# Decay sums of the scan: broadcast by transfers instead of by TensorE

## The reference

```python
a_cs = jnp.cumsum((dt * a).reshape(b, c, t, g, e), axis=2)
seg = a_cs[:, :, :, None] - a_cs[:, :, None, :]
decay = jnp.exp(jnp.where(lower, seg, -jnp.inf))
cb = jnp.einsum('bclgn,bcsgn->bclsg', Cc, Bc)
y_diag = jnp.einsum('bclsge,bcsgep->bclgep', cb[..., None] * decay, X)
y_off = jnp.einsum('bclgn,bcgepn->bclgep', Cc, s_in) * jnp.exp(a_cs)[..., None]
```

## Time and profile before

| | us |
|---|---|
| median of 3 runs | 1684.28 |
| all runs | 1684.26 to 1684.72 |
| profiled execution | 1684.64 |
| its span | 1682.9 |
| PE busy | 1659.0 |
| DVE busy | 1001.9 |
| ACT busy | 679.8 |
| POOL busy | 687.4 |

### The profile page before, as it was taken

The page is one execution under the profiler, slowest core; times in us unless marked ns, Lnnn a source line. Parts: engine busy times, 40 slices in busy tenths (PEclk is TensorE's granted clock), DMA queues, the critical chain, the costliest instruction groups (busy, mean ns, idle before and its releaser), DMA issues.

```text
span 1682.9 us, 20420 instructions
## 1 busy us (share of the span) xinstructions
PE 1659.0 (99%) x8004; PEld 1316.8 (78%) x8004; DVE 1001.9 (60%) x1387; ACT 679.8 (40%) x932; POOL 687.4 (41%) x339
## 2 busy tenths in 40 slices
PE   7999999999999999999999999999999999999999
PEld 5777787878778888888877777788777788888887
DVE  5589859778774545422236898596788654545100
ACT  5445553344443333332244555533543433333221
POOL 3432223233445555554443222232334455555443
PEclk9999999999999999999999999999999999999999
DMA  5532111212223232322224221112123223222233
GB/s 167 129 96 74 62 63 63 76 63 64 87 88 100 88 100 88 100 92 94 91 88 126 85 73 63 63 63 76 63 66 96 89 88 100 89 100 90 93 99 107
DMA packets 43231, 147.34 MB, mean 88 GB/s; under 512 B 5152, under 2 KB 5920, under 8 KB 43136
## 3 DMA queue, kind: packets, MB, share of 16 engines
q1 hardware_dynamic: 42752, 145.28, 26.9%
q0 software_dynamic: 384, 0.75, 0.4%
HBM read 143.17 MB, written 2.85 MB: 87 GB/s over the span
## 4 chain that ended last, share of the span: by engine, by line
PE 89%; DVE 6%; issue 2%; ACT 1%; POOL 1%; DMA 0%; SPq 0%; DVEq 0%
PE banks L1080 27%; PE banks L1082 26%; PE banks L1081 26%; PE banks L1172 2%; PE banks L1151 2%; PE banks L1160 2%; PE banks L1255 1%; DVE sb_w_lo L747 1%; PE banks L1268 1%; PE banks L1227 1%; PE banks L1131 1%; DVE sb_e L822 1%; PE banks L1241 1%; PE banks L1211 0%; DVE sb_squares L735 0%
## 5 line engine op out<-in xcount | busy, mean ns | idle before, releaser
L360 POOL TENSOR_TENSOR sb_w_lo<-sb_w_raw,sb_w_hi 128x1024 fp32r<-128x1024 f32 x202 | 490.4, 2428 | 633.1 <-ACT sb_w_hi L453 633.1
L1080 PE MATMUL banks<-sb_h_hi,sb_w_hi 128*128 128x512 f32 x1360 | 558.2, 410 | 16.1 <-POOL sb_w_lo L360 10.7
L453 ACT ACTIVATE sb_w_hi<-sb_w_raw 128x1024 fp32r<-128x1024 f32 x258 | 272.6, 1057 | 671.4 <-PE banks L1082 665.1
L1082 PE MATMUL banks<-sb_h_hi,sb_w_lo 128*128 128x512 f32 x1360 | 537.3, 395 | 0.0
L1081 PE MATMUL banks<-sb_h_lo,sb_w_hi 128*128 128x512 f32 x1360 | 537.1, 395 | 0.0
L1080 PEld LDWEIGHTS banks<-sb_h_hi,sb_w_hi 128*128 128x128 f32 x1360 | 256.5, 189 | 99.5 <-issue 36.9
L1081 PEld LDWEIGHTS banks<-sb_h_lo,sb_w_hi 128*128 128x128 f32 x1360 | 256.9, 189 | 61.8 <-issue 6.9
L1082 PEld LDWEIGHTS banks<-sb_h_hi,sb_w_lo 128*128 128x128 f32 x1360 | 256.5, 189 | 60.1
L1045 DVE TENSOR_TENSOR banks<-banks,sb_rstd 128x512 f32<-128x512 f32 x88 | 61.5, 699 | 144.0 <-PE banks L1082 135.7
L1080 PE MATMUL banks<-sb_ff_hi,sb_w_hi 128*128 128x512 f32 x352 | 138.9, 395 | 0.0
L1082 PE MATMUL banks<-sb_ff_hi,sb_w_lo 128*128 128x512 f32 x352 | 138.9, 395 | 0.0
(11 more groups left out here) (199 smaller groups left out, 2326.9 us busy)
## 6 DMA issues: line engine op xcount, KB each, us to landing
sb_w_raw<-w_in SPq DMA_DIRECT2D x88, 512.0 KB, 3.4
sb_w_raw<-w_up SPq DMA_DIRECT2D x88, 512.0 KB, 3.3
sb_w_raw<-w_out SPq DMA_DIRECT2D x32, 512.0 KB, 3.4
sb_w_raw<-w_down SPq DMA_DIRECT2D x32, 512.0 KB, 3.3
sb_bias_t<-bias_rows SPq DMA_DIRECT2D x16, 448.0 KB, 6.0
sb_w_raw<-w_down SPq DMA_DIRECT2D x16, 384.0 KB, 3.0
sb_x_stream<-x_t SPq DMA_DIRECT2D x4, 512.0 KB, 6.7
out_t<-sb_x_stream SPq DMA_DIRECT2D x8, 256.0 KB, 3.5
```

The lines of the kernel that those rows point to most:

```text
L360: g.tensor_tensor(WLO[:, n % 2, :], W[:, n % 2, :], WHI[:, n % 2, :].bitcast(F32), ALU.subtract).then_inc(w_lo.handle, 1)
L453: sc.activation(WHI[:, n % 2, :], W[:, n % 2, :], ACT.Copy).then_inc(w_hi.handle, 1)
L1080: mm(out, whi, hhi, start=start, stop=False)
L1082: return mm(out, wlo, hhi, start=False, stop=stop)
```

## The change

The rows of sums (and, exponentiated once by ScalarE for all heads, their exponentials) are stored to a buffer in HBM, `sum_rows`, at slot 4 of SyncE's order. SyncE then reads each head's two rows back into all 128 partitions of `head_e(h)` (`head_rows`, 512 KB), behind the weights of the slot two further on, and for each pair the exponentials of its four rows, each into 64 partitions of `EA` (`pair_exps`, two transfers of 192 KB). `row_sums` and its matmuls go, and with them the selectors, the high and low parts of the sums, and the exponential of L606. `seg` becomes eight operations of 128 columns, one for each direction and chunk, each of which subtracts the chunk's column and bounds in one. `HEAD_E` gets a fourth buffer, made of two pieces of 2 KB.

```diff
-    HEAD_E = (E[:, 0, :, :], E[:, 1, :, :], SQ[:, :, :])
+    HEAD_E = (E[:, 0, :, :], E[:, 1, :, :], SQ[:, :, :], rm["spread"][:, 0:16:15, :])
...
+        def store_rows():
+            sp.wait_ge(*cs_row.at(1))
+            sp.dma_start(sum_rows[0, :, :], T[0:2 * DIR, 0, :]).then_inc(rows_stored.handle, 16)
+            sp.wait_ge(*cs_exp.at(1))
+            sp.dma_start(sum_rows[1, :, :], ER[0:2 * DIR, :]).then_inc(rows_stored.handle, 16)
+
+        def head_rows(h):
+            grp, n = h // 8, h % 8
+            if h == 0:
+                sp.wait_ge(*rows_stored.at(32))
+                sp.wait_ge(*at_pv.at(UNITS))
+            if n % 4 == 2:
+                sp.wait_ge(*st_mm.at(6 * grp + 6))
+            if h == 3:
+                sp.wait_ge(*cb_mm.at(1))
+            if h >= 4:
+                sp.wait_ge(*y_mm.at(2 * ((h - 4) // 2) + 2))
+            rows = bass.AP(sum_rows.tensor, h * SEQ, [[0, P], [DIR * SEQ, 2], [1, SEQ]])
+            sp.dma_start(head_e(h), rows).then_inc(rows_landed[h % 4].handle, 16)
+
+        def pair_exps(t):
+            if t >= 2:
+                sp.wait_ge(*y_read.at(t - 1))
+            for d in range(2):
+                rows = bass.AP(sum_rows.tensor, (2 * DIR + DIR * d + 2 * t) * SEQ + (P, 0)[d], [[SEQ, 2], [0, 64], [1, SEQ - P]])
+                sp.dma_start(EA[:, t % 2, d, :], rows).then_inc(ea_landed[t % 2].handle, 16)
...
+                slot = pos - POS["sc", 0]
+                if slot == 4:
+                    store_rows()
+                if slot - 2 in ROWS_AT:
+                    head_rows(ROWS_AT[slot - 2])
+                if slot - 1 in PAIR_AT:
+                    pair_exps(PAIR_AT[slot - 1])
...
-                    act.wait_ge(*seg_read.at(h + 1))
-                    if h >= 4:
-                        act.wait_ge(*y_read.at(h // 2 - 1))
-                    sc.activation(EA[half, (h // 2) % 2, :, :].rearrange("p d l -> p (d l)"),
-                                  BANK[half, 2:4, :].rearrange("p b s -> p (b s)")[:, P:P + 768], ACT.Exp).then_inc(ea_done.handle, 1)
...
-                    sc.activation(CS[0:64, :], BANK[0:64, 2, :], ACT.Copy).then_inc(cs_hi.handle, 1)
+                    sc.activation(ER[0:64, :], BANK[0:64, 2, :], ACT.Exp).then_inc(cs_exp.handle, 1)
...
         def seg(h):
...
-            v.tensor_tensor(head_e(h).rearrange("p d (c l) -> p d c l", l=P),
-                            BANK[:, 2:4, :].rearrange("p d (c l) -> p d c l", l=P), columns, ALU.subtract).then_inc(seg_read.handle, 1)
-            dve.wait_ge(*seg_read.at(h + 1))
-            v.tensor_scalar(head_e(h), head_e(h), 80.0, None, ALU.min).then_inc(seg_done.handle, 1)
+            dve.wait_ge(*rows_landed[h % 4].at(16 * (h // 4 + 1)))
+            for d in range(2):
+                for c in range(QT):
+                    at = slice(P * c, P * c + P)
+                    ins = v.tensor_scalar(head_e(h)[:, d, at], head_e(h)[:, d, at], AS[:, c, column(d, h):column(d, h) + 1], 80.0,
+                                          ALU.subtract, ALU.min)
+            ins.then_inc(seg_done.handle, 1)
...
-            dve.wait_ge(*ea_done.at(2 * t + 2))
+            dve.wait_ge(*ea_landed[t % 2].at(32 * (t // 2 + 1)))
...
-                    dve.wait_ge(*cs_hi.at(1))
-                    v.tensor_tensor(CS[64:128, :], BANK[0:64, 2, :], CS[0:64, :].bitcast(F32), ALU.subtract).then_inc(cs_lo.handle, 1)
...
-                if k == KT // 2 and head is not None:
-                    row_sums(head)
...
-        def row_sums(h):
...
-            for d in range(2):
-                ins = mm(bank(2 + d), SEL[:, column(d, h):column(d, h) + 1].to_broadcast([P, P]), CS[:, :], start=True, stop=True)
-            ins.then_inc(ab_mm.handle, 1)
```

More of the change, by code:

```diff
@@ L159, in build_trunk @@
     con = {n: CON[:, i, :] for i, n in enumerate(CONSTS)}
-    SEL = sb("selectors", [P, 64], F32R)
     PAR = sb("params", [P, DEPTH, PA_N])
@@ L195, in build_trunk @@
                 ("x_tok", 40, [P, QT, 512], F32), ("s_in", 48, [P, 2, 3, SEQ], F32), ("b_tok", 60, [P, QT, P], F32),
-                ("cs", 62, [P, SEQ], F32R), ("exp_cs", 64, [P, 2, 2, 384], F32), ("cb", 70, [P, 2, SEQ], F32),
+                ("exp_rows", 62, [P, SEQ], F32), ("spread", 32, [P, 16, SEQ], F32), ("exp_cs", 64, [P, 2, 2, 384], F32), ("cb", 70, [P, 2, SEQ], F32),
                 ("e", 74, [P, 2, 2, SEQ], F32), ("mh_sc", 82, [P, 4, SEQ], F32R), ("ml_sc", 90, [P, 4, SEQ], F32R),
@@ L208, in build_trunk @@
     QHI, QLO, KHI, KLO = (rm[n] for n in ("q_high", "q_low", "k_high", "k_low"))
-    XT, SIN, BT, CS, EA, CB, E = (rm[n] for n in ("x_tok", "s_in", "b_tok", "cs", "exp_cs", "cb", "e"))
-    HEAD_E = (E[:, 0, :, :], E[:, 1, :, :], SQ[:, :, :])
+    XT, SIN, BT, ER, EA, CB, E = (rm[n] for n in ("x_tok", "s_in", "b_tok", "exp_rows", "exp_cs", "cb", "e"))
+    HEAD_E = (E[:, 0, :, :], E[:, 1, :, :], SQ[:, :, :], rm["spread"][:, 0:16:15, :])
     SCC, CX, SCA, SCP, Z = (rm[n] for n in ("sc_c", "sc_cx", "sc_acc", "sc_prod", "z"))
@@ L228, in build_trunk @@
     scratch = nc.dram_tensor("bias_rows", [HEADS, COPIES, REL], F32).ap()
+    sum_rows = nc.dram_tensor("sum_rows", [2, 2 * DIR, SEQ], F32).ap()
     con_landed, setup_landed = sem("con_landed"), sem("setup_landed")
@@ L233, in build_trunk @@
     x_stored = sem("x_stored")
-    sel_done, eps_done = sem("sel_done"), sem("eps_done")
+    eps_done = sem("eps_done")
+    rows_stored = sem("rows_stored", 32)
+    rows_landed = [sem(f"rows_landed{i}", 64) for i in range(4)]
+    ea_landed = [sem("ea_landed0", 128), sem("ea_landed1", 128)]
     bias_mm, bias_row = sem("bias_mm"), sem("bias_row")
@@ L258, in build_trunk @@
         sem(n, 1) for n in ("dt_tr", "dt_x", "dt_e", "dt_w", "dt_ln", "a_exp", "dt_done", "lndt_done", "da_done"))
-    cs_mm, cs_row, cs_hi, cs_lo, cs_tr, cs_col, dec_mm, dec_exp, ws_done = (
-        sem(n, 1) for n in ("cs_mm", "cs_row", "cs_hi_done", "cs_lo_done", "cs_tr", "cs_col", "dec_mm", "dec_exp", "ws_done"))
+    cs_mm, cs_row, cs_exp, cs_tr, cs_col, dec_mm, dec_exp, ws_done = (
+        sem(n, 1) for n in ("cs_mm", "cs_row", "cs_exp", "cs_tr", "cs_col", "dec_mm", "dec_exp", "ws_done"))
     tok_tr, tok_copied = sem("tok_tr", 10), sem("tok_copied", 10)
     cb_mm, cb_done, xs_done, st_mm, sin_done = sem("cb_mm", 2), sem("cb_done", 4), sem("xs_done", 12), sem("st_mm", 12), sem("sin_done", 12)
-    ab_mm, seg_read, seg_done, e_done, ea_done, g_done, y_mm = (
-        sem(n, SSD_HEADS) for n in ("ab_mm", "seg_read", "seg_done", "e_done", "ea_done", "g_done", "y_mm"))
+    seg_done, e_done, g_done, y_mm = (
+        sem(n, SSD_HEADS) for n in ("seg_done", "e_done", "g_done", "y_mm"))
     gs_done = sem("gs_done", SSD_HEADS // 2)
@@ L270, in head_e @@
     def head_e(h):
-        return HEAD_E[h % 8 % 3]
+        return HEAD_E[h % 4]
     def par(col, n=1):
@@ L601, in _ @@
                     h = ROWS_AT[s]
-                    half = slice(64 * (h % 2), 64 * (h % 2) + 64)
-                    act.wait_ge(*seg_read.at(h + 1))
-                    if h >= 4:
-                        act.wait_ge(*y_read.at(h // 2 - 1))
-                    sc.activation(EA[half, (h // 2) % 2, :, :].rearrange("p d l -> p (d l)"),
-                                  BANK[half, 2:4, :].rearrange("p b s -> p (b s)")[:, P:P + 768], ACT.Exp).then_inc(ea_done.handle, 1)
                     act.wait_ge(*seg_done.at(h + 1))
@@ L710, in setup @@
         def setup():
-            dve.wait_ge(con_landed.handle, 16)
-            v.tensor_tensor(SEL[:, :], con["ident"][:, 0:64], con["ident"][:, 64:128], ALU.add).then_inc(sel_done.handle, 1)
             for r in range(2):
@@ L855, in state_in @@
                 return
-            if grp:
-                dve.wait_ge(*t_read.at(4))
+            dve.wait_ge(*(t_read.at(4) if grp else rows_stored.at(32)))
             col = 64 + column(d, 8 * grp)
@@ L1103, in block_of, with tile @@
                 ins.then_inc(w_used.handle, 1)
-        def tile(kind, i, width=P, head=None):
+        def tile(kind, i, width=P):
             for k in range(KT):
-                if k == KT // 2 and head is not None:
-                    row_sums(head)
                 block_of(kind, i, k, width)
@@ L1197, in to_tokens @@
                 pe.wait_ge(*y_read.at(4))
-                pe.wait_ge(*ea_done.at(8))
-                pe.wait_ge(*seg_done.at(8))
             else:
-                pe.wait_ge(*cs_lo.at(1))
+                pe.wait_ge(*cs_exp.at(1))
                 pe.wait_ge(*cs_row.at(1))
@@ L1270, in from_states, with output_first @@
             ins.then_inc(yo_mm.handle, 1)
-        def output_first(m, head):
+        def output_first(m):
             s, b = weights("o1", m), tile_bank("o1", m)
             for k in range(KT):
-                if k == KT // 2 and head is not None:
-                    row_sums(head)
                 at = slice(P * k, P * k + P)
@@ L1345, in _ @@
                 if kind == "o1":
-                    output_first(i, ROWS_AT.get(s))
```

(3 more changed lines are left out.)

## The result

The changed kernel takes **1702.05 us** (median of 4 runs, 1700.33 to 1704.5) against 1684.3 for the kernel before on the same chip: ratio 1.0106, 95% interval 1.0088 to 1.0123. The change makes it slower, as forecast, but by 17.8 us where I had 9.0, and the time lies above the range (1673 to 1698). The profiled execution took 1700.33 us for a span of 1698.5, 15.6 more than before's 1682.9.

The account below looks back on a forecast made before the run. It took VectorE to run level with TensorE in the scans, so its work counts as much. Per layer -1.7 + 6.2 = +4.5 us, transfers 0, so +9.0 in all on 1684.64: 1693.6, put at 1693 us; range 1673 to 1698.

Parts of the forecast that it names:

- The passes, -15.0 us: Scans, TensorE: two matmuls a head fall away, 64 in all, 15.0 us over both layers, the most to win.
- VectorE runs level with TensorE: Scan stretches: VectorE arrives as TensorE needs it or up to 5 us before, so its work counts as much.
- `seg` at 1.68 us undisturbed: VectorE, each head: eight operations of 0.20 us plus a tail take 1.68 us, against 1.86 before.
- The port by turns: VectorE and GpSimd alternate by instruction, so eight short operations can lose a wait at each boundary; likeliest case, chance 0.48.
- slot 21 waiting for the z read-out: Group 1, TensorE: slot 21 waits for L1006's successor and starts at 376.9 us, four heads' gain gone.
- the walk: Old layer 0 times moved by the new seg: -1.7 us in group 0, +6.2 in group 1, +9.0 over both layers.
- head 15's `seg` at 7.55 us: End of group 1: beside four GpSimd operations it starts at 412.15 us and ends at 419.7.
- +6.2: Group 1, slot 25: `within` starts at 422.1 us instead of 415.93, 6.2 us later against the old course.
- The transfers: 23 MB of added reads of rows and exponentials: put at 0, at most 1 us a layer.
- a rival for rows that come late: Rows landing in 9 us or more stall heads 2 and 5: 1699 us; chance 0.10, shared with operations of 0.29 us.
- a draw: Rival: turns are taken but delays and gains nearly cancel, 1.4 to 4 us either way, about 1685 us; chance 0.14.

Follow-up runs that it names:

- e10: Kernel before, TensorE still making the rows, with subtraction and bound given to ScalarE as eight activations a head out of PSUM; 1680.24 us.
- e8: e1 with the eight short operations a head moved from VectorE to ScalarE, as relu that bounds the exponent at 8, not 80; 1666.57 us.
- e1: Changed kernel with each pair's exponentials read with the 64 copies as outermost dimension, not the two rows; 1689.26 us, ratio 1.0029.
- e6: e1 with only two of the eight short operations a head, the other six quarters left out; 1666.44 us.
- e5: Kernel before with TensorE's two matmuls a head for the rows of sums cut from 512 to 32 columns; 1681.63 us.
- e9: e1 with GpSimd's two additions of squares made to wait until the subtraction of head 15 is done; 1683.19 us, ratio 0.9994.
- e4: Kernel before, TensorE still making the rows, with seg as eight short VectorE operations reading PSUM; 1699.74 us, ratio 1.0089.

## Why the prediction was wrong

- **The passes, -15.0 us: right**, nearly in size too (13.7 between e10 and e8, with VectorE relieved in both).
- **"VectorE runs level with TensorE": right.** Relieving VectorE takes e1 from 1689.3 to 1666.4 us (e6), and in e5 more than half of what TensorE was spared came back as waits and clock.
- **`seg` at 1.68 us undisturbed: right** (1.66), and the start of each next one 0.2 us behind the last.
- **The port by turns: right as a mechanism** (e9), with the places: heads 9, 13, 15, and slot 21 waiting for the z read-out. **Its price, the walk's +9.0 us, was mis-sized**, too dark by some 9 us. It had head 15's `seg` at 7.55 us (6.61), and the end of head 13's moved by 3.85 where the operation itself grew by 3.45 - 1.66 = 1.8. In layer 0 of e1, where the rows come in time, group 1 lies 97.3 us behind group 0 (`within` of slot 13 to that of slot 25) against 94.2 before: +3.1 and not +6.2; from slot 2 to slot 13 it gains 2.6 us and not 1.7. By the walk the sum was +9.0; e1's span, +4.3, without its 4.6 us of clock has -0.3.
- **The transfers: this is the step that failed.** It read "I put it at 0, at most 1 us a layer"; it cost 12.8 us (e1), 15.6 in e8. I reckoned with bytes and a mean rate, and had a rival for rows that come late, decided at a landing of 7.7 us; they landed in 9.4. But I took the rows' own shape for the risk, and not the load ahead of them. The pair's pattern begins with a dimension of two, and moves 50 GB/s at a DMA share of 0.13, so its 384 KB take some 8 us. What SyncE issues behind it lands late (10.4 to 11.6 us for rows, 11.1 for weights), and with the pattern spread it does not (e1); that it waits on those two engines is the reading that fits, no view tells the engines apart. The Trainium skill, "DMA: Bandwidth & Descriptors", section "Rules for kernel authors", says that a transfer whose outermost dimension is smaller than sixteen runs on no more engines than that. The trace agrees: two of sixteen is 0.125, it shows 0.13. I had not weighed that rule against the diff's two lines.
- **The clock: left out.** I priced a stop of TensorE at its own length. With the stops of 3.97, 4.84 and 4.80 us it fell to the 1.2 GHz level, which cost 6.7 us beyond them in the changed kernel (2.1 of these inside the transfers' 12.8).

Added up: -0.3 (passes and turns, where I had +9.0) + 4.6 (clock in e1) + 12.8 (transfers, where I had 0) = 17.1, for 17.8 measured. The first term is what e1 leaves over, so this sum divides the time and does not prove it; the test is the account above. And it shows that "slower" was in part luck: of what I had priced, passes and turns, nothing is left (-0.3), a draw. Two terms that I had at nothing made the kernel slower, and the walk's error hid half of them.

The Trainium skill, "SBUF — State Buffer", section "SBUF: two separate sides", has the port pair as a lock held for a whole instruction. 6.61 us for 1.66 beside four operations agrees, and so does e4, whose reads from PSUM are never lengthened. That the other's queued instruction comes next, nearly each time, is what the rows add.

## What to carry to other kernels

Before a transfer is called free, read the first dimension of its pattern, and that of everything ahead of it in the same queue: a small one there delays large ones behind. When a train of short VectorE operations runs beside GpSimd, count the GpSimd operations in the row beside it, not its own length; taking two out of that row, or giving the train to ScalarE, is worth more than shortening it. And where an engine looks idle 40% of the time, walk the stretch that the change touches: the same 15 us of spared passes ended at -18 us with VectorE relieved (e8) and at +5 with it burdened (e1), both with the transfers spread.

## What was unexpected of the hardware

- TensorE at the 1.2 GHz level around a stop: the stops ahead of `within` of slot 25 are 4.84 us in the changed kernel and 4.2 in e1, and the clock falls to 0.50 before they end (420.4 of 422.16 us) or just behind them (416.2 for 415.6 us, layer 0 of e1); e9's are 2.2 us at most and it still loses 3.4 us. The kernel before, e8 and e10 lose none; their longest wait in the scans is about 1 us.
- A two-matmul pair of 32 columns takes 0.22 us where 512 columns take 0.46.
- Eight relu of 128 columns on ScalarE: 0.39 us long, 2.45 us for all eight, so 0.29 us apart; on VectorE 0.28 long and 0.20 apart. From PSUM the two engines are level: ScalarE's are 0.35 to 0.42 long and 0.25 apart (e10, 2.12 to 2.19 us for eight), VectorE's 0.34 long and 0.26 apart (e4, 2.15).
